# Rotary partners by ScalarE copies between partitions instead of permutation products on TensorE

## The reference

```python
def rotate(xp, ang):
    a, b = jnp.split(xp, 2, axis=-1)
    cos, sin = jnp.cos(ang), jnp.sin(ang)
    return jnp.concatenate([a * cos - b * sin, a * sin + b * cos], axis=-1)

def apply_axial_rope(x, ang_r, ang_c):
    xr, xc = jnp.split(x, 2, axis=-1)
    return jnp.concatenate([rotate(xr, ang_r), rotate(xc, ang_c)], axis=-1)

    # in retention_branch
    qh = apply_axial_rope(to_heads(q, RET_HEADS), ang_r, ang_c)
    kh = apply_axial_rope(to_heads(k, RET_HEADS), ang_r, ang_c) * kscale
```

## Time and profile before

| what | value |
|---|---|
| median of 3 runs | 3190.2 us |
| fastest run | 3189.81 us |
| highest run | 5469.89 us |
| profiled execution | 3190.06 us |
| its span | 3188.0 us |
| TensorE busy | 3070.2 us, 96% |
| VectorE busy | 1522.7 us, 48% |
| ScalarE busy | 743.9 us, 23% |
| GpSimd busy | 1183.1 us, 37% |
| mean granted TensorE clock | 0.992 |

### The profile page before, as it was taken

One profiled execution on the slowest core, in us unless ns is written; L12 is line 12 of the kernel. 1 busy time (PEld: TensorE's weight loads), 2 busy tenths in 40 slices (PEclk: granted clock), 3 DMA queues, 4 the chain that ended last, 5 costly groups with the idle time before them and its releaser, 6 DMA issues.

```text
span 3188.0 us, 40649 instructions
## 1 busy us (share of the span) xinstructions
PE 3070.2 (96%) x16864; PEld 2489.6 (78%) x16864; DVE 1522.7 (48%) x1729; ACT 743.9 (23%) x988; POOL 1183.1 (37%) x553
## 2 busy tenths in 40 slices
PE   6999998999999999999999999999899999999998
PEld 5877886788877787777767788778688888888877
DVE  3134508428743432925676502442763155155477
ACT  2011215302232122511554301122211001000132
POOL 2232230026642323036643344444244434444442
PEclk9999999999999999999999999999999999999999
DMA  6200111233231011113411111112211111111211
GB/s 247 73 28 14 33 43 43 97 132 132 67 137 33 15 34 51 64 60 99 148 64 40 40 46 51 43 56 93 79 53 47 46 53 46 46 53 46 107 45 73
DMA packets 64283, 213.39 MB, mean 67 GB/s; under 512 B 6160, under 2 KB 7952, under 8 KB 64144
## 3 DMA queue, kind: packets, MB, share of 16 engines
q1 hardware_dynamic: 44256, 149.97, 14.4%
q10 hardware_dynamic: 19888, 61.39, 5.2%
HBM read 194.56 MB, written 16.78 MB: 66 GB/s over the span
## 4 chain that ended last, share of the span: by engine, by line
PE 67%; issue 12%; DVE 10%; POOL 6%; DMA 3%; ACT 2%; POOLq 0%; SPq 0%; DVEq 0%; ACTq 0%
PE ps L590 58%; DMA raw<-s 3%; DVE Sb L2045 3%; POOL w_hi L507 3%; POOL w_lo L509 3%; PE ps L901 2%; DVE C L2367 1%; PE ps L811 1%; PE ps L726 1%; PE ps L1117 1%; PE ps L817 0%; DVE g_lo L2462 0%; PE ps L833 0%; PE ps L788 0%; DVE st L2047 0%
## 5 line engine op out<-in xcount | busy, mean ns | idle before, releaser
L507 POOL TENSOR_TENSOR w_hi<-raw,pool_zero 128x1024 fp32r<-128x1024 f32 (+2 forms) x256 | 482.3, 1884 | 1909.3 <-PE ps L590 1770.0
L509 POOL TENSOR_TENSOR w_lo<-raw,w_hi 128x1024 fp32r<-128x1024 f32 (+2 forms) x256 | 666.0, 2602 | 20.1
L590 PE MATMUL ps<-g_hi,w_hi 128*128 128x512 f32 x1632 | 530.8, 396 | 11.7 <-DVE xc L2392 4.2
L590 PE MATMUL ps<-g_hi,w_lo 128*128 128x512 f32 x1632 | 521.4, 390 | 0.0
L590 PE MATMUL ps<-g_lo,w_hi 128*128 128x512 f32 x1632 | 521.4, 390 | 0.0
L590 PE MATMUL ps<-h_hi,w_hi 128*128 128x512 f32 (+1 forms) x1496 | 428.9, 378 | 6.6 <-POOL w_lo L509 4.6
L590 PE MATMUL ps<-h_hi,w_lo 128*128 128x512 f32 (+1 forms) x1496 | 408.9, 365 | 0.0
L590 PE MATMUL ps<-h_lo,w_hi 128*128 128x512 f32 (+1 forms) x1496 | 408.8, 364 | 0.0
L590 PEld LDWEIGHTS ps<-g_hi,w_hi 128*128 128x128 f32 x1632 | 307.0, 189 | 84.4 <-issue 10.2
L590 PEld LDWEIGHTS ps<-g_lo,w_hi 128*128 128x128 f32 x1632 | 307.8, 189 | 65.0 <-issue 0.7
L590 PEld LDWEIGHTS ps<-g_hi,w_lo 128*128 128x128 f32 x1632 | 307.4, 188 | 64.6
(11 more groups left out here) (367 smaller groups left out, 3529.0 us busy)
## 6 DMA issues: line engine op xcount, KB each, us to landing
raw<-s SPq DMA_DIRECT2D x239, 512.0 KB, 3.4
modring<-modw ACTq DMA_DIRECT2D x32, 512.0 KB, 4.6
modfirst<-modw SPq DMA_DIRECT2D x4, 1024.0 KB, 18.2
modfirst<-modw ACTq DMA_DIRECT2D x4, 1024.0 KB, 25.0
x_saved<-Y ACTq DMA_DIRECT2D x1, 4096.0 KB, 14.7
x_part<-x_saved ACTq DMA_DIRECT2D x2, 2048.0 KB, 10.1
x_saved<-Y ACTq DMA_DIRECT2D x2, 2048.0 KB, 8.5
B<-x_saved ACTq DMA_DIRECT2D x1, 4096.0 KB, 15.5
```

Source lines behind the costliest of these rows:

```text
L507: G.tensor_tensor(w_hi[s][:, :n], raw[s][:, :n], zero.to_broadcast([P, n]), ALU.add).then_inc(hi_done, 1)
L509: G.tensor_tensor(w_lo[s][:, :n], raw[s][:, :n], w_hi[s][:, :n].bitcast(F32), ALU.subtract)\
L590: last = T.matmul(ps[:, o + c0:o + c0 + size], wt[s][:, kk], xx[:, k, t0:t0 + size], start=(x == 0 and n == 0), stop=(x == k_n - 1 and n = ...
```

## The change

The partners are no longer made by a product. The weight splits of the query and key slabs write the 64 features of a head in another order, both a groups ahead of both b groups, so that a feature's partner stands 32 partitions away. ScalarE copies each quarter of 32 partitions of a chunk to the partitions of its partner in banks 6 and 7, four copies of 32x1024 a chunk, with the sign as the copy's scale. The rotary steps on VectorE are as before. The tables `cosT` and `sinT` are loaded in the new order, in eight DMAs instead of two. The loops over slabs on GpSimd are cut once more in each layer, after the sixth slab.

```diff
-            def split(s, k, g):
+            def split(s, k, g, apart=False):
                 n = k * P
-                G.tensor_tensor(w_hi[s][:, :n], raw[s][:, :n], zero.to_broadcast([P, n]), ALU.add).then_inc(hi_done, 1)
+                views = [raw[s][:, :n], w_hi[s][:, :n], w_lo[s][:, :n], zero.to_broadcast([P, n])]
+                if apart:
+                    views[0] = views[0].rearrange("p (x r h f) -> p h x r f", r=2, h=2, f=HD // 4)
+                    views[1:] = [v.rearrange("p (x h r f) -> p h x r f", r=2, h=2, f=HD // 4) for v in views[1:]]
+                    views = [[v[:, h] for v in views] for h in range(2)]
+                else:
+                    views = [views]
+                for weights, hi, lo, none in views:
+                    last = G.tensor_tensor(hi, weights, none, ALU.add)
+                last.then_inc(hi_done, 1)
                 pool.wait_ge(hi_done, g + 1)
-                G.tensor_tensor(w_lo[s][:, :n], raw[s][:, :n], w_hi[s][:, :n].bitcast(F32), ALU.subtract)\
-                    .then_inc(split_done, 1)
+                for weights, hi, lo, none in views:
+                    last = G.tensor_tensor(lo, weights, hi.bitcast(F32), ALU.subtract)
+                last.then_inc(split_done, 1)
...
-            for g0, turns, places in runs(CUTS):
+            for g0, turns, places in runs(CUTS + (6, LAYER_AT[1] + 6)):
...
-                        split(x % 2, k, g)
+                        split(x % 2, k, g, g0 in (0, G_HEAD, LAYER_AT[1]))
...
-                        if k == (7, 6, 5, 4, 3, 2)[c]:
-                            if l == 0 and c == 0:
-                                pe.wait_ge(mod_added, 5)
-                            rotate(c)
                         if c == 3 and k in (2, 5):
                             if k == 2:
                                 pe.wait_ge(evac_done, g0 + 9)
@@ -762,6 +760,7 @@
                             turn_values(6 * l + 2, 0)
                         if c == 5 and k == 6:
                             pe.wait_ge(vt_used, 6 * l + 3)
+                            pe.wait_ge(rope_done, 6 * l + 4)
...
-                act.dma_start(cosT[:], ropes[0]).then_inc(tab_in, 16)
-                act.dma_start(sinT[:], ropes[1]).then_inc(tab_in, 16)
+                for to, table in ((cosT, ropes[0]), (sinT, ropes[1])):
+                    by_half = table.rearrange("(a r h f) t -> a h r f t", a=2, r=2, h=2)
+                    for q in range(4):
+                        act.dma_start(to[32 * q:32 * q + 32, :], by_half[q // 2, q % 2]).then_inc(tab_in, 16)
...
+                def partners(c):
+                    act.wait_ge(evac_done, g0 + 6)
+                    if l == 0 and c == 0:
+                        act.wait_ge(mod_added, 5)
+                    act.wait_ge(rope_done, 6 * l + c + 1)
+                    for q in (32, 0, 96, 64):
+                        last = A.activation(ps[q ^ 32:(q ^ 32) + 32, 6 * BANK:8 * BANK], QK[q:q + 32, c, CTX:], ACT.Copy,
+                                            scale=-1.0 if q & 32 else 1.0)
+                    last.then_inc(rot_ready, 1)
...
+                    if c == 0:
+                        partners(0)
+                    elif c == 1:
+                        partners(3)
+                    else:
+                        partners(5)
                     evac_part(g0 + 7 + 2 * c, Y[:, 2 + c, :], ACT.Silu)
+                    if c == 1:
+                        partners(4)
...
+                        partners(1)
+                        partners(2)
```

More of the change, by code:

```diff
@@ L532, in _ @@
                         pool.wait_ge(raw_loaded[s], 16)
-                        split(s, KD, s)
+                        split(s, KD, s, True)
                 lo = 1 if g0 == 0 else 0
@@ L719, in turn_values @@
                     last.then_inc(vt_ready, 1)
-                def rotate(c):
-                    pe.wait_ge(tab_in, 48 * (l + 1))
-                    pe.wait_ge(rope_done, 6 * l + c + 1)
-                    for half in range(2):
-                        last = T.matmul(ps[:, (6 + half) * BANK:(7 + half) * BANK], ret_const[:, 0, :],
-                                        QK[:, c, CTX + 512 * half:CTX + 512 * (half + 1)], start=True, stop=True)
-                    last.then_inc(rot_ready, 1)
                 def turn_pair_keys(p, gi):
@@ L1108, in maps @@
                         return
-                    pe.wait_ge(tab_in, 112)
+                    pe.wait_ge(tab_in, 304)
                     pe.wait_ge(rnn_xc, c + 1)
@@ L1792, in _ @@
                     if f == FF_GROUPS - 1 and n == 2:
-                        act.wait_ge(tab_in, 160)
+                        act.wait_ge(tab_in, 352)
                         highs("p", 2, lambda k: p_raw[:, k, :], lambda k: p_hi[:, k, :], lambda k: None)
@@ L1929, in _ @@
                     dve.wait_ge(xs_out, 16)
-                dve.wait_ge(tab_in, 48 * (l + 1))
+                dve.wait_ge(tab_in, 144 * (l + 1))
                 for h in range(6):
@@ L2436, in _ @@
                 own.link(V.memset(buf[:, 0:16], 0.0))
-            dve.wait_ge(tab_in, 144)
+            dve.wait_ge(tab_in, 336)
             for c in range(4):
```

## The result

The changed kernel takes 3195.8 us (median of 12 runs), the kernel before 3189.8 us on the same chip: ratio 1.0019, 95% interval 1.0011 to 1.0027. That is **6 us slower** (3.5 to 8.6), where 14 us faster was forecast. The profiled execution has a span of 3191.9 us against 3188.0. One of the 12 runs of the kernel before took 5469.89 us, and two of the nine of experiment 1 took 5097.05 and 9944.86 us; the medians and ratios here are without such runs. Each ratio is against runs of the kernel before on the same chip, and the experiments stood on three chips, so between experiments the ratios are compared and not the medians.

The account below looks back on a forecast made before the run. TensorE, busy 96% of the span, was taken to bound the kernel. -20.6 + 1.0 + 2.9 + 0 + 1.0 + 1.6 = -14.1 us from 3190.06 gave 3176 us, range 3167 to 3185.

Parts of the forecast that it names:

- The rest, at nothing: Six more DMA issues on ScalarE delay layer 1's first evacuation by up to 2.8 us, covered by a split wait: 0 us.
- The products: Twelve `rotate` products leave TensorE's chain at 1.72 us each: 20.6 us off, the upper bound of the gain.
- ScalarE's set: Four partner copies of 32x1024 from SBUF to PSUM, 1.03 us each with small overlaps: 3.85 us a set.
- (b): Rival: dearer copy sets, through partition crossing or PSUM written a quarter at a time; 3182 to 3198 us, chance 9%.
- (1): Each layer's last copy set delays the first own score (L788): 1.0 us on in layer 0, 2.9 in layer 1.
- (3): TensorE's clock falls after a 4.2 us rest ahead of L788 in layer 1: 1.0 us on, bounds 0 and 1.2.
- (2): `partners(2)` ahead of the second value slab's evacuation: 0 us, no cover left in layer 1, 0.9 us in layer 0.
- GpSimd's halves: 18 splits written as two halves cost 0.3 us more each; 1.6 us exposed where TensorE waits for splits.
- (c): Rival: GpSimd's strided reads make such splits take twice their time; 3201 us, 11 slower than before, chance 6%.
- (a): Rival: the order of edits hides the late sets and the clock stays up; 3171 or 3169.5 us, chance 14%.
- (d): Rival: another engine's wait replaces the product, 1.5 us a collision, three giving 3180 us; beyond 3181, chance 7%.
- anything else: Outcomes outside the forecast band and the four lettered rivals: chance 2%.

Follow-up runs that it names:

- experiment 1: The changed kernel with its rotary tables stored in the new order and loaded whole, two loads instead of eight: 3181.0 us, ratio 0.9978 to the kernel before.
- experiment 2: The kernel before with each table loaded in four plain pieces of 32 partitions, old order, eight issues instead of two: 3189.9 us, ratio 1.0002.
- experiment 8: As experiment 1, with each layer's last set of partner copies issued ahead of ScalarE's third value evacuation: 3177.1 us, ratio 0.9958 to the kernel before.
- experiment 9: The kernel before with only GpSimd's 18 splits written as two patterned halves each (not the reference's attention inputs): 3193.8 us, ratio 1.0015.
- experiment 10: As experiment 8, with the six splits of the second layer's head written whole (not the reference's output): 3172.2 us, ratio 0.9946 to the kernel before.
- experiment 11: As experiment 8, with four throwaway products of 384 columns on TensorE in the rest ahead of layer 1's third slab: 3172.7 us, ratio 0.9949.
- experiment 4: The changed kernel with its eight patterned table loads issued behind the evacuations of slabs 0 and 1: 3196.2 us, ratio 1.0025 to the kernel before.

## Why the prediction was wrong

**The step that failed** is "The rest, at nothing": "Six more DMA issues of up to 0.46 us put off layer 1's first evacuation by up to 2.8 us". It priced the pieces as plain loads, looked at layer 1 only and named the right cover there; for plain pieces it holds (experiment 2). But the source of each is two separated groups of 16 rows, and while such loads ran, the share of two of 16 DMA engines was busy (0.12 to 0.13), an issue took up to 2.65 us and the issues behind were held as well. Measured between the changed kernel and experiment 1: 13 us, spread over a wait of 9.2 us in layer 0 and one of 7.6 us in layer 1, each in place of a shorter one on the split. "The table bytes are the same" was true and the wrong measure. With this term at nothing, as in experiment 1, the range (3167 to 3185) holds the 3181.0, but the gain is 7 us and not 14: the other terms were too small by as much.

The other terms, with what experiments 1, 8, 9 and 10 measured. They add up: -19.8 for the products, +8.2 for the late sets and the clock behind them and +4.8 for the splits give -6.8, where experiment 1 has -7.0; with the 13.1 of the table loads it is +6.3, where the changed kernel has +6.

- **The products, -20.6.** Right: experiment 8 shows 10.2 and 9.6 us off in the two stretches once nothing is late.
- **ScalarE's set, 3.85 us.** Measured 4.12: each copy 1.02 us and no overlap. The prediction took one of 0.09 us from small operations and quoted one of 93 ns beside it; neither is seen between these copies, which start 1.03 us apart. The 1.02 is as forecast. (b) is out.
- **(1) The last sets, +1.0 and +2.9, and (3) the clock, +1.0.** The rest in layer 1 is 4.53 us (forecast 4.2). In layer 0 TensorE rests 2.6 us, and the clock falls there as well, which the prediction didn't have at all: L832 takes 3.75 us in the changed kernel and 2.32 in experiment 8. Together experiment 8 gives 8.2 us back where 4.9 were put on. The clock was mis-sized, and above its bound of 1.2. Against experiment 1, of the 2.7 us that the early set saves in layer 0, 1.3 are the rest and 1.4 the clock; of the 5.5 in layer 1, 3.2 are the rest and 2.3 the clock.
- **(2) The second value slab, 0.** Right but for 0.5 us: in the changed kernel TensorE waits 0.49 us for it in layer 1.
- **GpSimd's halves, +1.6.** Uncontended it is 0.3 us a split, as worked out, with no room for a cost of the patterned reads, so (c) with its doubled splits is out. Exposed it was 4.8 us (experiment 9). The term held only the added instructions. It missed that the halves stretch beside VectorE in the head (2.5 us), where two low halves take 1.9 us each, near the 2 us that the prediction named as the sign of (c); a part of (c) may hide there. And it missed that with 0.3 us more of rest in layer 1 (2.12 for 1.83) the clock fell (1.4 us).
- **The chances.** The cases (a) to (d) all were about the copies, the splits and the order; none had the table loads. The 2% for "anything else" was far too little for a part that had been priced in one sentence.

## What to carry to other kernels

When a load's access pattern changes, count the outermost dimension before the bytes: with two groups in the source 0.12 of the DMA engines was busy here, and the engine that issued the loads was held too. A constant table should be stored in the order in which it is used. And when a wait is lengthened by tenths of a microsecond, look what TensorE's clock does behind it: here four throwaway products in the rest gave 1.4 us, more than the 0.3 by which the rest had grown.

## What the runs showed of the hardware that was not expected

- Busy share of the DMA engines by outermost count of the source, loads of 32 rows of 4 KB each in layer 0: 2: 0.12 to 0.13 and 41 to 53 GB/s; 4: 0.24 to 0.25 and 88 to 98; 8: 0.41 to 0.43 and 123 to 141; 16: 0.65 to 0.67 and 201 to 205.
- A plain load issued behind them from the same engine pays too: `ret_const` took 2.26 and 4.06 us to issue, and 0.45 us where the tables came whole.
- ScalarE's 32-partition copies from SBUF to other partitions in PSUM cost the same as evacuations of 128 partitions: 1.02 us for 1024 columns, start to start 1.03.
- After a rest of 1.83 us TensorE's granted clock stayed at 1.00 at the third slab of layer 1; after 2.12 us at the same place it was 0.50 (1.2 GHz) for some 3 us, and with the rest filled (experiment 11) it stayed at 1.00. The length of the rest isn't all there is to it: after 2.11 us in experiment 4 it stayed at 1.00 as well.
- GpSimd's splits and VectorE's norm slow each other where they overlap: a split's low part took 2.40 us alone (median) and 3.00 beside the norm as one instruction, some 2.53 and 3.85 as two.
